# Two blocks on one core: the up products of 36 expert tiles in the routing and spreading stages, a spreading of 16 tokens and six banks, and the context's modulation of 16 tiles

## The reference

```python
def peer(h, w_pq, sub_keys, expert_u, expert_v):       # h: 512 tokens of 1024
    q = (xb @ w_pq).reshape(PEER_BLOCK, PEER_HEADS, 2, PEER_DKH)      # 8 heads, 2 halves of 128
    s = einsum('thpd,hpkd->thpk', q, sub_keys)                        # 128 keys a half
    sv, si = lax.top_k(s, PEER_TOPK)                                  # 16 best of each half
    cand = sv[:, :, 0, :, None] + sv[:, :, 1, None, :]
    cidx = si[:, :, 0, :, None] * N_KEYS + si[:, :, 1, None, :]
    best, pos = lax.top_k(cand, PEER_TOPK)                            # 16 experts of 16384
    eidx = take_along_axis(cidx, pos)
    g = softmax(best)
    act = gelu(einsum('thkd,td->thk', expert_u[eidx], xb), approximate=False)
    return einsum('thk,thkd->td', g * act, expert_v[eidx])

mod_ctx = s_cc @ w_ada[l] + b_ada[l]                     # 6 * 1024 numbers
csh1, csc1, cgt1, csh2, csc2, cgt2 = split(mod_ctx, 6)   # of these only csh1 and csc1 are used here
```

## Time and profile before

| what | value |
|---|---|
| median of 3 runs | 4464.96 us (4459.31 to 4465.61) |
| the profiled execution, its own time | 4457.59 us |
| its span, first to last instruction | 4455.9 us |
| mean granted clock of PE | 0.932 |
| busy: PE, DVE, ACT, POOL | 3667.2, 2714.8, 1487.4, 463.4 us |
| second gated MLP, first up product to last down product | 1981.1 to 2410.0 us |
| routing, first product to last transpose | 2931.3 to 3159.4 us |
| spreading, first one-hot to last copy | 3162.4 to 3338.9 us |
| experts, first up product to start of the last down product | 3366.9 to 4442.6 us |

### The profile page before, as it was taken

How to read it: one execution, slowest core, us unless ns; L and a number is a source line. 1 busy time by engine, 2 the same in 40 slices (tenths; PEclk the granted TensorE clock), 3 DMA queues, 4 the chain that set the end, 5 groups by cost and what they waited for, 6 DMA issues and landing times. The chain is left out here.

```text
span 4455.9 us, 52480 instructions
## 1 busy us (share of the span) xinstructions
PE 3667.2 (82%) x17647; PEld 3039.5 (68%) x17647; DVE 2714.8 (61%) x5515; ACT 1487.4 (33%) x2569; POOL 463.4 (10%) x456
## 2 busy tenths in 40 slices
PE   0688899699958889968887978954466999999999
PEld 0566777588746677757665836743356999999998
DVE  6566524377556552437775565469995666667676
ACT  1344434232234443422222343321233333333332
POOL 0000000101000000011001200221001222222222
PEclk9899999899989999989988988976798999999999
DMA  7211122245121112224431200020158777777775
GB/s 297 76 50 39 43 71 85 95 179 198 66 77 47 42 43 67 84 89 172 155 123 59 70 5 5 29 70 17 49 142 289 268 278 290 263 272 284 264 285 206
DMA packets 259644, 583.87 MB, mean 131 GB/s; under 512 B 116080, under 2 KB 135280, under 8 KB 256880
## 3 DMA queue, kind: packets, MB, share of 16 engines
q1 hardware_dynamic: 208320, 395.09, 25.3%
q0 software_dynamic: 51120, 186.14, 12.0%
HBM read 551.55 MB, written 29.62 MB: 130 GB/s over the span
## 5 line engine op out<-in xcount | busy, mean ns | idle before, releaser
L313 PE MATMUL ps<-mix_w,mix_h 128*128 128x384 f32 (+1 forms) x2304 | 535.4, 382 | 93.8 <-DVE mix_w L726 74.2
L2819 PE MATMUL ps<-peer_h,peer_u 128*128 128x384 f32 x3072 | 559.8, 337 | 37.8 <-DVE peer_u L2917 28.8
L2819 PEld LDWEIGHTS ps<-peer_h,peer_u 128*128 128x128 f32 x3072 | 542.6, 189 | 48.0 <-DVE peer_u L2917 29.0
L313 PEld LDWEIGHTS ps<-mix_w,mix_h 128*128 128x128 f32 x2304 | 422.5, 195 | 197.7 <-DVE mix_w L726 82.0
L2830 PE MATMUL ps<-peer_v,peer_coef 128*128 128x512 f32 x2304 | 547.8, 391 | 0.0
L2830 PEld LDWEIGHTS ps<-peer_v,peer_coef 128*128 128x128 f32 x2304 | 430.6, 188 | 85.3
L1084 PE MATMUL ps<-mix_h,mlp_u 128*128 128x512 f32 x1536 | 367.7, 401 | 122.9 <-DVEq L1180 122.8
L1084 PEld LDWEIGHTS ps<-mix_h,mlp_u 128*128 128x128 f32 x1536 | 298.3, 195 | 191.2 <-DVEq L1180 127.9
L1095 PE MATMUL ps<-mlp_coef,mlp_v 128*128 128x512 f32 x1536 | 354.3, 392 | 19.5 <-DVEq L1191 19.5
L726 DVE TENSOR_TENSOR mix_w<-mix_raw,mix_w 128x1024 fp32r<-128x1024 f32 (+1 forms) x164 | 185.4, 1145 | 278.5 <-ACT mix_w L526 277.6
L1095 PEld LDWEIGHTS ps<-mlp_coef,mlp_v 128*128 128x128 f32 x1536 | 290.5, 189 | 81.0 <-DVEq L1191 20.3
(11 more groups left out here) (506 smaller groups left out, 5948.1 us busy)
## 6 DMA issues: line engine op xcount, KB each, us to landing
peer_raw_u<-in_u_tiles SPq DMA_DIRECT2D x128, 512.0 KB
peer_raw_v<-in_v_tiles SPq DMA_DIRECT2D x128, 512.0 KB, 14.8
mlp_tiles<-in_w_ada POOLq DMA_DIRECT2D x96, 512.0 KB, 4.4
mix_raw<-in_w_rest SPq DMA_DIRECT2D x68, 512.0 KB, 3.6
mlp_raw_u<-in_w_up SPq DMA_DIRECT2D x64, 512.0 KB, 9.2
mlp_raw_v<-in_w_down SPq DMA_DIRECT2D x16, 2048.0 KB, 8.1
set_ring<-in_w_ada SPq DMA_DIRECT2D x48, 512.0 KB, 8.6
mix_raw<-in_w_a SPq DMA_DIRECT2D x48, 512.0 KB, 4.0
```

The source lines that it names most:

```text
L313: last = pe.matmul(proj(u, n_cols), M.H[:, x, k, b * P:(b + 1) * P], V.w[:, y, i % SLOTS_W, k % 2 * n_cols:(k % 2 + 1) * n_cols], start=k ...
L2819: last = pe.matmul(bank(M.ps, 6 + t % 2, DENSE), Q.u[:, x, t % 4, k * P:(k + 1) * P], Q.h[:, y, k, 0:DENSE], start=k + n == 0, stop=k == K ...
```

## The change

* **MLP.** The loop of six groups becomes one of two groups with `side.conds` and one of four with `side.conds[:1]`. So the context's row is multiplied with 16 tiles and no longer with 48; the bias addition at the start of block two is cut to fit.
* **Early tiles.** 36 of the 128 expert tiles (`EARLY`: 3, 7, 10, 14, 17, 21, 24, 28, ..., 127) have their up product and GELU made before the experts stage, 24 in the routing and 12 in the spreading. The result of each (128x384) is stored in HBM (`early_dram`, 192 KB) and loaded again as `Q.act` when its turn comes. In both stages the low word of `u` is made on POOL. Four more tiles of `u` (0, 1, 2, 4) are loaded and split in the spreading stage, and their products made in the experts stage.
* **Spreading.** The loops are written out. DVE writes `hot_i` of four tokens in one `tensor_tensor` of 128x512 with broadcast operands, `hot_j` as before; rings of 16 tokens; six banks. The wait for the last stores moves into the experts stage, on SyncE ahead of the first load of weights.
* **Experts.** 92 up products; PE's order is ups(0), ups(1), ups(2), then for every t downs(t), and ups(t+4) if that tile isn't an early one. DVE's and ACT's work is likewise made one or two tiles earlier. Several buffers get other places.

In the diff, cut to its core, BOTH is 2, BEHIND is 4, AHEAD is 4, EARLY_ROUTE is 24, TURNS is 48, and `tiles` in the spreading are 12 early tiles and tiles 0, 1, 2 and 4.

```diff
-            with dve.Fori(0, GROUPS - 2) as g:
+            with dve.Fori(0, BOTH) as g:
                 low_coef(g)
                 scales(g + 1, True, g)
-                adds(g, True)
+                adds(g, side.conds)
+                step.again()
+            with dve.Fori(BOTH, GROUPS - 2) as g:
+                low_coef(g)
+                scales(g + 1, True, g)
+                adds(g, side.conds[:1])
                 step.again()
...
 def route_stage(nc, M, Q, d, early_dram):
...
         def _(sp):
+            def load_u(e):
+                if e >= 4:
+                    sp.wait_ge(u_low, e - 3)
+                sp.dma_start(Q.early_raw[:, e % 4], d["u_tiles"][EARLY[e]]).then_inc(u_here[e % 4], 16)
+            def keep(e):
+                sp.wait_ge(opened, e + 1)
+                sp.dma_start(early_dram[e], Q.early_act[:, e % 2]).then_inc(M.early_kept[e % 2], 16)
             for j in range(H2):
...
                 sp.dma_start(Q.raw[:, j % RING], d["w_pq"][j]).then_inc(raw_here[j % RING], 16)
+                if j >= 1:
+                    load_u(j - 1)
+                if j >= 9:
+                    keep(j - 9)
...
+            for e in range(H2 - 9, EARLY_ROUTE):
+                if e + 8 < EARLY_ROUTE:
+                    load_u(e + 8)
+                keep(e)
...
         def _(pe):
+            def ups(e):
+                pe.wait_ge(u_low, e + 1)
+                if e >= 2:
+                    pe.wait_ge(opened, e - 1)
...
                 if j:
                     scores(j - 1)
+                if j >= BEHIND:
+                    ups(j - BEHIND)
             scores(H2 - 1)
+            ups(H2 - BEHIND)
...
             last.then_inc(natural_done, 1)
+            for e in range(H2 - BEHIND + 1, EARLY_ROUTE):
+                ups(e)
+            pe.wait_ge(opened, EARLY_ROUTE)
             pe.wait_ge(picked, 1)
...
         def _(act):
+            def high_u(e):
+                act.wait_ge(u_here[e % 4], 16 * (e // 4 + 1))
+                if e >= 3:
+                    act.wait_ge(u_done, e - 2)
+                act.copy(Q.early_u[:, HI, e % 3], Q.early_raw[:, e % 4]).then_inc(u_high, 1)
+            def activate(e):
+                act.wait_ge(u_done, e + 1)
+                if e >= 2:
+                    act.wait_ge(M.early_kept[e % 2], 16 * (e // 2))
+                act.activation(Q.early_act[:, e % 2], bank(M.ps, 6 + e % 2, DENSE), ACT.Gelu).then_inc(opened, 1)
...
             act.wait_ge(natural_done, 1)
             step(act.copy(Q.natural[:, :], M.ps[:, 0:D]))
+            for e in range(H2 - BEHIND + 1, EARLY_ROUTE):
+                activate(e)
+                if e + 3 < EARLY_ROUTE:
+                    high_u(e + 3)
             act.wait_ge(levelled, 1)
...
 def spread_stage(nc, M, Q, d, spread_dram, early_dram):
...
+            for q in range(2 * TURNS):
+                if q >= 4:
+                    dve.wait_ge(hots_used, q - 3)
+                at = q % 4 * 4
+                dve.tensor_tensor(Q.hot_i[:, at:at + 4], Q.iota128[:, :].unsqueeze(1).broadcast_to([P, 4, P]),
+                                  Q.pickT[:, 0, q * 4:q * 4 + 4].unsqueeze(2).broadcast_to([P, 4, P]),
+                                  ALU.is_equal).then_inc(hots, 1)
+                for n in range(4):
+                    t = q * 4 + n
+                    dve.tensor_scalar(Q.hot_j[:, at + n], Q.iota128[:, :], Q.pickT[:, 1, t:t + 1], Q.pickT[:, 2, t:t + 1],
+                                      ALU.is_equal, ALU.mult).then_inc(hots, 1)
...
+            for e in range(len(tiles)):
+                pool.wait_ge(u_high, e + 1)
+                pool.tensor_tensor(Q.u[:, LO, e % 4], Q.raw_u[:, e % 4], Q.u[:, HI, e % 4],
+                                   ALU.subtract).then_inc(u_low, 1)
...
-            for side in range(2):
-                sp.wait_ge(kept[side], 16 * BLOCKS + 16)
...
+            for i in range(AHEAD, 2 * AHEAD):
+                load_u(i)
+            for side in range(2):
+                sp.wait_ge(M.kept[side], 16 * (DENSE // P))
+                sp.wait_ge(M.early_kept[side], 8 * len(EARLY))
             load_weights(0)
...
-            ups(0)
-            ups(1)
+            for t in range(4):
+                if plain(t):
+                    ups(t)
             for t in range(NT):
-                if t + 2 < NT:
-                    ups(t + 2)
                 downs(t)
+                if plain(t + 4):
+                    ups(t + 4)
```

More of the change, by code:

```diff
@@ L989, in gated_mlp_stage @@
     SLOTS = E.slots
+    BOTH = 2
     with stage(nc, *[f"u_here{j}" for j in range(G)],
@@ L2716, in _ @@
                     for n in range(4):
-                        j = half * 4 + n
-                        last = pe.matmul(M.ps[:, half * BANK + n * P:half * BANK + (n + 1) * P], Q.hot_i[:, j],
-                                         Q.hot_j[:, j], start=True, stop=True)
+                        last = pe.matmul(M.ps[:, q % 6 * BANK + n * P:q % 6 * BANK + (n + 1) * P],
+                                         Q.hot_i[:, q % 4 * 4 + n], Q.hot_j[:, q % 4 * 4 + n], start=True, stop=True)
                     last.then_inc(hots_used, 1)
+                e, part = divmod(g, EACH)
@@ new lines, in _ @@
+                if part == 0:
+                    pe.wait_ge(u_low, e + 1)
+                    if e >= 2:
+                        pe.wait_ge(opened, e - 1)
+                for k in range(part * KB // EACH, (part + 1) * KB // EACH):
+                    for n, (x, y) in enumerate(PASSES):
+                        last = pe.matmul(bank(M.ps, 6 + e % 2, DENSE), Q.u[:, x, e % 4, k * P:(k + 1) * P],
+                                         Q.h[:, y, k, 0:DENSE], start=k + n == 0, stop=k == KB - 1 and n == 2)
@@ new lines, in activate @@
+            def activate(e):
+                act.wait_ge(u_done, e + 1)
+                if e >= 2:
+                    act.wait_ge(M.early_kept[e % 2], 16 * ((EARLY_ROUTE + e) // 2))
+                act.activation(Q.late_act[e % 2], bank(M.ps, 6 + e % 2, DENSE), ACT.Gelu).then_inc(opened, 1)
+            for e in range(3):
+                high(e)
+            for n in range(2):
+                act.wait_ge(M.early_kept[n], 8 * EARLY_ROUTE)
+            for q in range(2 * TURNS):
+                block_of, at = divmod(q * 4, P)
+                side, at = divmod(at, HALF_T)
+                if at == 0 and block_of:
+                    act.wait_ge(M.kept[side], 16 * block_of)
+                act.wait_ge(hots_used, q + 1)
+                act.copy(Q.table[:, side, :, at:at + 4],
+                         bank(M.ps, q % 6).rearrange("p (t j) -> p j t", t=4)).then_inc(laid, 1)
+                e, part = divmod(q, 2 * EACH)
+                if part == 0:
+                    if e >= 1:
+                        activate(e - 1)
+                    high(e + 3)
@@ L2740, in _ @@
+            activate(EARLY_SPREAD - 1)
+            for e in range(EARLY_SPREAD + 3, len(tiles)):
+                high(e)
         @block.sync
         def _(sp):
-            for side in range(2):
-                sp.sem_inc(kept[side], 16)
-            with sp.Fori(0, BLOCKS) as b:
-                for side in range(2):
-                    sp.wait_ge(stored, b * 2 + (side + 1))
-                    sp.dma_start(spread_dram.rearrange("j i t -> i j t")[:, :, bass.ds(b * P + side * HALF_T, HALF_T)],
-                                 Q.table[:, side, :, :]).then_inc(kept[side], 16)
@@ L2749, in _, with load, keep @@
-            for side in range(2):
-                sp.wait_ge(kept[side], 16 * BLOCKS + 16)
-def experts_stage(nc, M, Q, d, spread_dram, rows_here, out):
+            def load(e):
+                if e >= 4:
+                    sp.wait_ge(u_low, e - 3)
+                sp.dma_start(Q.raw_u[:, e % 4], d["u_tiles"][tiles[e]]).then_inc(raw_here[e % 4], 16)
+            def keep(e):
+                sp.wait_ge(opened, e + 1)
+                sp.dma_start(early_dram[EARLY_ROUTE + e], Q.late_act[e % 2]).then_inc(M.early_kept[e % 2], 16)
```

266 lines of the change are left out of this document (161 added, 105 removed).

## The result

The changed kernel takes **4339.5 us** (median of 4 runs, 4336.3 to 4342.9), the kernel before beside it 4465.3 us: ratio 0.972, 95% interval 0.970 to 0.974. That is inside the range given (4255 to 4350), but 4.5 us above the forecast's own range (4265 to 4335) and 37 us above the number forecast: the change gives 126 us by the medians where 163 were forecast. The profiled execution took 4342.0 us, 115.6 us less than the one of before (4457.6). Of all runs one is left out of its median, a run of e5 that took 13354.7 us at a granted clock of 0.556 where the kernel's three others had 0.94.

A forecast was written before the change was run, and what follows sets the result against it. The prediction took PE to bound the experts, DVE the routing and spreading. Its terms, -151 - 45 + 36 + 10 - 13 = -163 us, took 4457.6 to 4294.6, plus 7.4 gave 4302 us; range 4255 to 4350, the forecast's own 4265 to 4335.

The forecast's parts named there:

- Experts, steady part: Experts stage, bound by PE: 36 fewer up products of 4.19 us behind the first down product, -151 us.
- The doubt that landing times would grow: Rival for the experts: loads of `v` land slower and set the pace; at 34 us landing 4570 us, chance 1%.
- MLP: Second MLP: four groups with one row less, 11.3 us each, -45 us.
- Routing: Routing stage: added early tiles cost time at its end, the port and the `w_pq` loads; +36 us, between +8 and +60.
- The port: Routing: POOL's 24 more subtractions hold DVE's operations with two SBUF tensors, a quarter of its time; 5 us.
- The tail: Routing's end: GELUs 12 to 17 come 7.5 us apart through SyncE's queue, so the exponential is 31 us late.
- Spreading: Spreading stage: merged `hot_i` gains, POOL's subtractions and stores cost; +10 us, between -15 and +30.
- The merged `hot_i`: Spreading: `hot_i` of four tokens in one DVE operation, 1.63 us a quartet in place of 1.81; -17 us.
- POOL: Spreading: POOL's 16 subtractions each make DVE's `hot_i` wait about 1.6 us, +25 us.
- Start of the experts: From last spreading product to first down product: first three ups run under the 4 MB store; -13 us (-20 to -5).
- the 7.4 us between profiled execution and median: The profiled execution before lay 7.4 us under the median; added to 4294.6 to forecast the median.
- B: Rival for routing and spreading: each of POOL's 40 new subtractions holds DVE, 83 us; 4347 us, chance 17%.

The follow-up runs named there:

- e5: e2 with the spreading's 16 low words made by DVE in place of POOL: 4293.1 us, ratio 0.963.
- e9: e5 with 24 early tiles in the routing and 16, not 12, in the spreading: 4296.1 us, ratio 0.964.
- e1: The kernel before with only the change's MLP part and the cut bias addition: 4418.3 us, ratio 0.990.
- e10: e5 with 20 early tiles, not 24, in the routing and 16, not 12, in the spreading: 4297.6 us, ratio 0.963.
- e3: The changed kernel without POOL's low words for the 24 early tiles of the routing: 4304.6 us, ratio 0.964.
- e2: The changed kernel with SyncE issuing an early tile's store ahead of the next load in the routing's tail: 4309.5 us, ratio 0.965.
- e8: e2 with no early tile in the spreading, its 12 given back to the experts: 4327.7 us, ratio 0.970.
- e6: e2 with the spreading's last early tile stored through POOL's queue, and first weights and `v` loaded ahead of four `u` tiles: 4307.8 us, ratio 0.966.

## Why the prediction was right, and where it was not

1. **Experts, steady part: right.** -151 predicted, -150.2 measured; PE full in the windows. The doubt that landing times would grow was unfounded, they fell. e9 shows how near the edge was: four tiles more shortened the down products by 1.4 us and not 16.8.
2. **MLP: right.** -45 predicted; -44.3 in the change's trace with the way to the routing, -42.1 by e1's medians. The same stretch is 39 to 41 us shorter in the profiles of e1 to e10, so some us of it go with the profile; the groups' pace is the forecast's in all that are shown.
3. **Routing: the failing step**, +36 predicted with +60 as its upper bound, +62.5 measured; 26 of the 47 us that the sum was short.
   - *The port* was put at 5 us and cost 21.8 us up to the last score copy. I counted only DVE's instructions with two SBUF tensors as held, a quarter of its time. The time for which DVE was held there rose from 2.1 to 24.7 us. The rows show `TENSOR_SCALAR` and `CAST` held too, and worse, the meetings are not by chance: POOL's two subtractions follow each other, and DVE, held by the first, meets the second as it comes free. e3 is the proof: without the early tiles' low words 15.4 us went. The rule that would have told me stands in the Trainium skill (SBUF — State Buffer, "Who interferes with whom"): copy, cast and tensor_scalar can enter modes that use both port pairs and so contend with GpSimd, and a reduction never does. The trace agrees: in the change's routing and spreading five TENSOR_REDUCE start while POOL subtracts, and none is lengthened; of `CAST`, `TENSOR_SCALAR` and instructions with two SBUF tensors 28 start so, and all are (in e1 to e10, 190 of 197). MAX8, FIND_INDEX8 and MATCH_REPLACE8 aren't held either, none of 145. I cited the same page for its lock and not this list.
   - *The tail* was put at +31, measured +40.6. The mechanism was right, turn by turn, and e2 removes it. Its size was off: six turns of 8.7 us and not 7.5, +7 us, and the first turn begins 3.9 us behind the score copy.
4. **Spreading: right within its range**, +10 predicted, +13.7 measured, by two parts. The merged `hot_i`: -17 predicted, and e8's quartet of 1.63 us is the forecast's to the digit. POOL: 25 predicted, 31 measured, 2.06 us for each of 15 meetings and not 1.6 for 16. The step erred in who is held: not `hot_i` behind 1 us of `hot_j` that may pass, but `hot_j`, so nothing passes.
5. **Start of the experts:** -13 predicted, -8.8 measured, in its range. Not named: the issue of the last small store took 17.3 us behind the 4 MB store, so the plain ups did not run under it. But e6 shows that this was not what cost the 4 us. By the terms of the sum: to the first weights' issue 23.3 us (21 for the store), from there to ACT's cast of the second `v` tile 18.2 (13 for the loads), splitting and scaling 4.1 (5). So it was the loads that were put too low, with `u` ahead of them in the queue; e6's order brought them to 14.7, and its later landing of the store took that back.
6. **Not in the sum:** +7.8 ahead of the second MLP, where e1 to e10 stand 2.8 us earlier to 4.8 us later than before and the change latest of all, so that it is put down to the profile and not explained; and +4.0 at the end, where the shorter stage waits for the last gathered rows.

The errors: routing 26, spreading 4, start 4, end 4, ahead of the second MLP 8, MLP 1, experts 1: 48 us against a sum that gave 4294.6 for the profiled execution; it took 4342.0. By the medians it is 37, since the 7.4 us between profiled execution and median, which I added, did not recur: here the profiled execution stands 2.5 us above its median. Of the rivals B was nearest, 4347 us, and its mechanism is in part the one that worked: POOL holds DVE nearly each time in the spreading, 15 of 16, but in 14 of 40 subtractions in the routing, for what DVE runs there is mostly free of it. It had been given 17%; its 83 us were too many (58 measured in both stages) and its tail too small. Its number is also not what its words give: 33 us for the spreading and half of the routing's 50 are 58, 28 above the sum's 30 and not 45, so 4330 us. That 4347 lies so near is luck.

## What to carry to other kernels

Before giving POOL work beside a full VectorE, list which of VectorE's instructions POOL can hold, here casts and tensor_scalar as well as those with two SBUF tensors, and count each meeting at nearly POOL's whole instruction (2.06 of 2.38 us here); if VectorE can do the piece in less time than POOL holds it, as here 1.23 against 2.1 us, let it. In a queue issued in order, put the store that frees a buffer ahead of the load that waits for an engine: that one move was worth 30 us, where the whole change gave 126. And work moved out of a bound stage is worth its time there only until the next engine is reached; that point, here between 36 and 40 tiles, belongs in the sum.
